# Output projection of an encoder block: seven half-size products in place of eight

## What is computed

```
y_ml = mlstm_group(q, k, v, o, ig, fg)            # [256, 1024]
y_ssm = mamba2_group(z, xbc, dt)                  # [256, 1024], normalised in 4 groups
mix = concat([y_ml, y_ssm], -1) @ w_out           # [256, 2048] @ [2048, 1024]
h = layer_norm(ALPHA * x + mix, ln1_g, ln1_b)
out = layer_norm(ALPHA * h + moe(h), ln2_g, ln2_b)
```

## Time and profile before

| | us |
|---|---|
| median of 3 runs | 746.25 (745.76 to 746.35) |
| profiled execution, span from its first to its last instruction | 744.0 |
| runs' median less that span (what lies around it) | 2.25 |
| TensorE busy | 713.8 (96%) |
| VectorE / ScalarE / GpSimd busy | 260.9 / 165.0 / 48.0 |
| data moved | 251.01 MB, 337 GB/s over the span |

### The profile page before, as it was taken

The page is one execution under the profiler, slowest core; times in us unless marked ns, Lnnn a source line. Parts: engine busy times, 40 slices in busy tenths (PEclk is TensorE's granted clock), DMA queues, the critical chain, the costliest instruction groups (busy, mean ns, idle before and its releaser), DMA issues.

```text
span 744.0 us, 11161 instructions
## 1 busy us (share of the span) xinstructions
PE 713.8 (96%) x4514; PEld 416.7 (56%) x4518; DVE 260.9 (35%) x639; ACT 165.0 (22%) x345; POOL 48.0 (6%) x65
## 2 busy tenths in 40 slices
PE   7999999999999999999999999999998999999993
PEld 6888888888864455445444435444443445444441
DVE  3401599657757085222112211022211122112225
ACT  1010423407940043111111111111111121111111
POOL 0120020320320020100000000000000000000000
PEclk9999999999999999999999999999999999999997
DMA  8964544544398548999999999999999999999993
GB/s 335 406 209 142 177 164 169 179 161 165 119 385 364 226 173 344 357 370 425 424 420 430 424 430 432 427 428 422 432 427 427 425 426 423 425 424 424 418 404 134
DMA packets 30946, 251.01 MB, mean 337 GB/s; under 512 B 4000, under 2 KB 4800, under 8 KB 10032
## 3 DMA queue, kind: packets, MB, share of 16 engines
q1 hardware_dynamic: 27792, 240.78, 79.4%
q0 software_dynamic: 2448, 8.48, 3.2%
q10 hardware_dynamic: 656, 1.05, 0.4%
HBM read 249.31 MB, written 1.11 MB: 337 GB/s over the span
## 4 chain that ended last, share of the span: by engine, by line
PE 72%; DMA 10%; DVE 9%; SPq 6%; issue 1%; ACT 1%; DVEq 0%
PE bank L1212 20%; PE bank L820 16%; DMA arena<-in_we_dram 10%; PE bank L1280 8%; PE bank L963 7%; PE bank L1131 7%; DVE arena L1603 5%; PE bank L1149 4%; SPq L627 3%; PE bank L934 1%; PE bank L900 1%; SPq L636 1%; PE bank L1254 1%; PE bank L1289 1%; ACT bank L1368 1%
## 5 line engine op out<-in xcount | busy, mean ns | idle before, releaser
L1212 PE MATMUL bank<-arena 128*64 128x512 f32 (+2 forms) x1008 | 198.8, 601 | 5.4 <-DMA arena<-in_we_dram 5.4
L820 PE MATMUL bank<-arena 128*128 128x256 f32 x768 | 167.7, 379 | 0.0
L820 PEld LDWEIGHTS bank<-arena 128*128 128x128 f32 x768 | 145.6, 190 | 20.5 <-issue 0.4
L1212 PEld LDWEIGHTS bank<-arena 128*64 128x64 f32 (+2 forms) x1008 | 57.7, 127 | 96.6 <-issue 94.0
L1280 PE MATMUL bank<-arena 128*64 128x512 f32 (+2 forms) x512 | 91.7, 584 | 3.5 <-DMA arena<-in_we_dram 2.1
L1131 PEld LDWEIGHTS bank<-onehotb,h_part 128*128 128x128 bf16 x1200 | 67.2, 98 | 19.4 <-issue 19.4
L1131 PE MATMUL bank<-onehotb,h_part 128*128 128x128 bf16 x1200 | 71.3, 219 | 0.0
L1928 DVE TENSOR_TENSOR y_lo<-bank,y_hi 128x512 fp32r<-128x512 f32 (+1 forms) x51 | 34.7, 681 | 101.9 <-ACT y_hi L1513 75.5
L1905 DVE TENSOR_REDUCE arena<-bank 64x1 f32<-64x3 f32 (+1 forms) x64 | 10.1, 158 | 160.8 <-PE bank L1230 160.2
L1280 PEld LDWEIGHTS bank<-arena 128*64 128x64 f32 (+1 forms) x512 | 26.3, 124 | 54.0 <-issue 44.6
L963 PE MATMUL bank<-arena 128*128 128x512 f32 x128 | 55.3, 592 | 0.0
(11 more groups left out here) (276 smaller groups left out, 493.6 us busy)
## 6 DMA issues: line engine op xcount, KB each, us to landing
arena<-in_we_dram SPq DMA_DIRECT2D x82, 1024.0 KB, 19.6
arena<-in_we_dram SPq DMA_DIRECT2D x17, 3072.0 KB, 30.8
arena<-in_we_dram SPq DMA_DIRECT2D x22, 2048.0 KB, 31.4
arena<-in_wc_dram SPq DMA_DIRECT2D x15, 1024.0 KB, 11.2
arena<-in_wn_dram SPq DMA_DIRECT2D x8, 1024.0 KB, 4.7
arena<-in_wo_dram SPq DMA_DIRECT2D x8, 1024.0 KB, 4.8
apart<-in_we_dram SPq DMA_DIRECT2D x7, 1024.0 KB, 29.7
arena<-decay_rows POOLq DMA_DIRECT2D x5, 1024.0 KB, 7.1
```

What stands on the lines that cost most here:

```text
L820: mm = nc.tensor.matmul(bank[n % 2][:, j * S:(j + 1) * S], wk, xk, start=(k == 0), stop=(k == KD - 1))
L1212: mm = nc.tensor.matmul(bank[0][rows[q], :], hc[v][:, k, rows[q]], place[at_q[part][q]][:, c:c + 512], start=(k == 0), stop=(k == KD - 1))
```

## The change

Each unit is read as a 2 x 2 block product: tokens' blocks A11, A12 (row block 0 and 1 of token block 0), A21, A22 (token block 1), and weight blocks B11, B12, B21, B22 (row block by column half). Seven products, each summed over the units in a bank of its own, take the place of the eight, in Winograd's form of Strassen's scheme: 1 = A11 B11, 2 = A12 B21, 3 = S4 B22, 4 = A22 T4, 5 = S1 T1, 6 = S2 T2, 7 = S3 T3.

GpSimd forms T1 to T4 (`weight_sums`): for units 0 and 1 between decay families 3 and 4, for 2 and 3 after families 3 and 4, for 4 to 7 behind the iota, each when unit m - 4 has been used. VectorE forms S1 to S4 (`token_sums`) for the mLSTM units before the variances and for the Mamba units before `layer_norm`, where the results are put together from the banks. TensorE's order: products 1 and 2 of units 0 to 3, the first sum of squares, the other five products unit by unit with the second sum of squares behind unit 0, then for units 4 to 7 product by product in the order 1, 2, 6, 5, 3, 7, 4.

The sums lie in places 20, 21, 8 and 15, so that those aren't loaded ahead of the projection's end; units 4 to 7 are loaded when product 3 is done.

```diff
+PROD = {1: bank[0], 2: bank[1], 3: bank[2], 4: bank[3], 5: bank[6], 6: bank[4], 7: bank[7]}
+ML_U = OUNITS // 2
+SUM_PLACES = (20, 21, 8, 15)
+sums_at = [place[i] for i in SUM_PLACES]
+DONE = {p: ML_U + 1 + i for i, p in enumerate((1, 2, 6, 5, 3, 7, 4))}
+def b_parts(m):
+    w, t = unit[m], sums_at[m % ML_U]
+    return ([w[:, i * 512:(i + 1) * 512] for i in range(4)], [w[:, 512:1024]] + [t[:, i * 512:(i + 1) * 512]
+                                                                               for i in range(3)])
+def a_sum(m, i):
+    return sums_at[m % ML_U][:, 1536 + (i - 1) * P:1536 + i * P]
+def a_part(m, block, t):
+    y = yT if m < ML_U else xbc
+    return y[:, 2 * m + block, t * P:(t + 1) * P]
...
     assert [home(STATIC_AT[c // 6], None, c % 6 // 2, c % 2) for c in range(PLACES)] == list(range(PLACES))
-    for c in range(20, PLACES):
-        load_first(c)
-    sp.wait_ge(decay_exp, 4 * NB)
-    load_first(8)
     sp.wait_ge(ssm_ready, 3)
     load_first(14)
     sp.wait_ge(ssm_ready, 4)
     load_first(13)
-    sp.wait_ge(decay_exp, FAMS * NB)
-    load_first(15)
     sp.wait_ge(y_ready, 1)
     load_first(16)
     load_first(19)
-    for u in range(4):
+    for u in range(ML_U):
         sp.wait_ge(mix_used, u + 1)
         load_first(u)
     load_first(12)
     sp.wait_ge(y_ssm, G)
     load_first(17)
-    sp.wait_ge(mix_used, 5)
-    load_first(4)
-    sp.wait_ge(mix_used, OUNITS)
-    for u in range(5, RING_U):
+    sp.wait_ge(mix_used, DONE[3])
+    for u in range(ML_U, OUNITS):
         load_first(u)
+    sp.wait_ge(mix_used, DONE[4])
+    for c in sorted(SUM_PLACES):
+        load_first(c)
     sp.wait_ge(h_ready, 2 * T)
     load_first(10)
     sp.wait_ge(logit_ready, T)
...
-    for fam in range(3, FAMS):
-        pool.wait_ge(decay_exp, (fam - 1) * NB)
-        decay_rows(fam)
+    pool_chain = [0]
+    def pool_link(ins):
+        ins.then_inc(s_pool, 1)
+        pool_chain[0] += 1
+        pool.wait_ge(s_pool, pool_chain[0])
+    def weight_sums(m):
+        u = CUNITS + RUNITS + m
+        pool.wait_ge(unit_full[u % RING_U], 16 * (u // RING_U + 1))
+        (b11, b12, b21, b22), (t1, t2, t3, t4) = b_parts(m)
+        pool_link(nc.gpsimd.tensor_tensor(t3, b22, b12, ALU.subtract))
+        pool_link(nc.gpsimd.tensor_tensor(t1, b12, b11, ALU.subtract))
+        pool_link(nc.gpsimd.tensor_tensor(t2, b22, t1, ALU.subtract))
+        nc.gpsimd.tensor_tensor(t4, t2, b21, ALU.subtract).then_inc(b_sums, 1)
+    pool.wait_ge(decay_exp, 2 * NB)
+    decay_rows(3)
+    weight_sums(0)
+    weight_sums(1)
+    pool.wait_ge(decay_exp, 3 * NB)
+    decay_rows(4)
     pool.wait_ge(rows_masked, 4 * FAMS)
     nc.gpsimd.tensor_scalar(nidentb, identb[:], -1.0, None, ALU.mult).then_inc(consts_ready, 1)
+    pool.wait_ge(decay_exp, 4 * NB)
+    weight_sums(2)
+    pool.wait_ge(decay_exp, FAMS * NB)
+    weight_sums(3)
     pool.wait_ge(ssm_ready, G)
     pool.dma_start(at(O_XPAD, 2 * D), a["ln"][:, 0:2 * D].to_broadcast([P, 2 * D])).then_inc(s_late, 16)
     for g in range(G):
...
+        weight_sums(m)
     halves = [slice(0, 512), slice(512, D)]
...
     for half in range(2):
         c = halves[half]
         pool.wait_ge(h_part1, 1 + half)
...
-    def project(k, t, halves=(0, 1)):
...
-    for m in range(4):
+    def squares(m):
+        if m == 0:
+            pe.wait_ge(consts_ready, 1)
+            pe.wait_ge(misc_evac, M_SQ)
+        else:
+            pe.wait_ge(misc_evac, M_SQ + 1)
+        pe.wait_ge(sq_sum, 2 * m + 2)
+        for i in range(2):
+            mm = nc.tensor.matmul(bank[5][:, i * S:(i + 1) * S], ones, zT[:, 4 * m + 2 * i, :],
+                                  start=True, stop=True)
+        mm.then_inc(misc_ready, 1)
+    def product(p, m):
+        (b11, _, b21, b22), (t1, t2, t3, t4) = b_parts(m)
+        by = {1: b11, 2: b21, 3: b22, 4: t4, 5: t1, 6: t2, 7: t3}[p]
+        y = {1: a_part(m, 0, 0), 2: a_part(m, 1, 0), 3: a_sum(m, 4), 4: a_part(m, 1, 1), 5: a_sum(m, 1),
+             6: a_sum(m, 2), 7: a_sum(m, 3)}[p]
+        return nc.tensor.matmul(PROD[p][:, :], y, by, start=(m == 0), stop=(m == OUNITS - 1))
+    for m in range(ML_U):
         y_transpose(m)
     pe.wait_ge(proj_evac, ZSTEP + 3)
+    for m in range(ML_U):
+        u = CUNITS + RUNITS + m
+        pe.wait_ge(unit_full[u % RING_U], 16 * (u // RING_U + 1))
+        pe.wait_ge(misc_evac, M_Y + m + 1)
+        for p in (1, 2):
+            product(p, m)
+    squares(0)
     pe.wait_ge(weight_ready, 5 * NB)
-    for k in range(SPLIT_K):
-        for t in range(T):
-            mm = project(k, t)
-        if k % 2 == 1:
-            mm.then_inc(mix_used, 1)
-        if k == SQUARES_AFTER:
-            pe.wait_ge(consts_ready, 1)
-            pe.wait_ge(sq_sum, G)
-            for m in range(2):
-                ps = misc(M_SQ + m)
-                for i in range(2):
-                    mm = nc.tensor.matmul(ps[:, i * S:(i + 1) * S], ones, zT[:, 4 * m + 2 * i, :],
-                                          start=True, stop=True)
-                mm.then_inc(misc_ready, 1)
-    for t, halves in ((0, (0, 1)), (1, (0,)), (1, (1,))):
-        for k in range(SPLIT_K, 2 * KD):
-            mm = project(k, t, halves)
+    pe.wait_ge(ssm_read, G)
+    for m in range(ML_U):
+        pe.wait_ge(b_sums, m + 1)
+        product(4, m)
+        if m == 0:
+            pe.wait_ge(y_ready, 2)
+        for p in (3, 5, 6):
+            product(p, m)
+        product(7, m).then_inc(mix_used, 1)
+        if m == 0:
+            squares(1)
+    for p in (1, 2, 6, 5, 3, 7, 4):
+        if p == 6:
+            pe.wait_ge(y_ready, 3)
+        for m in range(ML_U, OUNITS):
+            if p == 1:
+                u = CUNITS + RUNITS + m
+                pe.wait_ge(unit_full[u % RING_U], 16 * (u // RING_U + 1))
+                pe.wait_ge(y_ssm, m - ML_U + 1)
+            if p == 6:
+                pe.wait_ge(b_sums, m + 1)
+            mm = product(p, m)
         mm.then_inc(mix_used, 1)
     def transposes(t):
...
+    def token_sums(units):
+        for m in units:
+            ins = V.tensor_tensor(a_sum(m, 1), a_part(m, 0, 1), a_part(m, 1, 1), ALU.add)
+        link(ins)
+        for m in units:
+            V.tensor_tensor(a_sum(m, 3), a_part(m, 0, 0), a_part(m, 0, 1), ALU.subtract)
+        for m in units:
+            ins = V.tensor_tensor(a_sum(m, 2), a_sum(m, 1), a_part(m, 0, 0), ALU.subtract)
+        link(ins)
+        for m in units:
+            ins = V.tensor_tensor(a_sum(m, 4), a_part(m, 1, 0), a_sum(m, 2), ALU.subtract)
+        ins.then_inc(y_ready, 1)
+    dve.wait_ge(misc_evac, M_Y + 4)
+    token_sums(range(ML_U))
...
                         ).then_inc(misc_evac, 1)
     dve.wait_ge(misc_evac, M_SQ + 2)
     dve.wait_ge(y_gated, G)
...
+        h11, h12, h21, h22 = [h[:, t, n * 512:(n + 1) * 512] for t in range(T) for n in range(2)]
+        def from_x(to, t, n, by):
+            return V.scalar_tensor_tensor(out=to, in0=xin[:, t, n * 512:(n + 1) * 512], scalar=ALPHA, in1=by,
+                                          op0=ALU.mult, op1=ALU.add)
+        def plus(to, p, op=ALU.add):
+            return V.tensor_tensor(to, to, PROD[p][:, :], op)
+        dve.wait_ge(mix_used, DONE[1])
+        link(from_x(h11, 0, 0, PROD[1][:, :]))
+        dve.wait_ge(mix_used, DONE[2])
+        link(plus(h11, 2))
+        V.bn_stats(stat[:, 0, :], h11)
+        dve.wait_ge(mix_used, DONE[6])
+        link(V.tensor_copy(pair_sum, PROD[1][:, :]))
+        link(plus(pair_sum, 6))
+        from_x(h12, 0, 1, pair_sum)
+        from_x(h21, 1, 0, pair_sum)
+        link(from_x(h22, 1, 1, pair_sum))
+        dve.wait_ge(mix_used, DONE[5])
+        plus(h12, 5)
+        link(plus(h22, 5))
         for t in range(T):
-            for half in range(2):
-                dve.wait_ge(mix_used, MIXED[t][half])
-                c = slice(half * 512, (half + 1) * 512)
-                link(V.scalar_tensor_tensor(out=h[:, t, c], in0=xin[:, t, c], scalar=ALPHA,
-                                            in1=bank[2 * t + half][:, :], op0=ALU.mult, op1=ALU.add))
-                link(V.bn_stats(stat[:, 2 * t + half, :], h[:, t, c]))
+            if t == 0:
+                dve.wait_ge(mix_used, DONE[3])
+                link(plus(h12, 3))
+                link(V.bn_stats(stat[:, 1, :], h12))
+            else:
+                dve.wait_ge(mix_used, DONE[7])
+                plus(h21, 7)
+                link(plus(h22, 7))
+                V.bn_stats(stat[:, 3, :], h22)
+                dve.wait_ge(mix_used, DONE[4])
+                link(plus(h21, 4, ALU.subtract))
+                link(V.bn_stats(stat[:, 2, :], h21))
             link(V.bn_aggr(mv[:, t, :], stat[:, 2 * t:2 * t + 2, :].rearrange("p a b -> p (a b)")))
             V.tensor_scalar(vv[:, 0, t:t + 1], mv[:, t, 1:2], EPS, None, ALU.add).then_inc(var_ready, 1)
             dve.wait_ge(var_ready, 2 + t)
...
```

(19 more changed lines are left out.)

## The result

The changed kernel takes 752.81 us (752.42 to 753.64, 4 runs) against 746.0 for the kernel before (744.27 to 746.35, 4 runs): 0.91% more by the medians, the ratio of the runs 1.0102 with an interval of 1.0086 to 1.0119. Slower, as forecast, but by 6.8 us where the forecast had 3.8, and 0.3 us above the upper end of its own range. The profiled execution's span is 751.2, against 744.0.

What follows compares the result with a forecast made beforehand. Expert-weight transfers were taken to pace the kernel, their start hanging on the projection. Work +3.2 and transfers +4.8 gave +3.8 on the 744.0 span: 747.8, plus 2.25 for timed runs: 750.0 us, range 748.0 to 752.5, chance 0.6.

Steps and rivals of the forecast that it cites:

- What bounds the kernel, and the sign: Expert weights pace the kernel from about 330 us; the end follows their stream's start and remaining bytes; slower, chance 0.69.
- The mechanism: GpSimd's last sixteen sums and VectorE's chain take turns; y_ssm complete at 250.5, TensorE idle about 8 us before unit 6.
- wait of 1 to 2 us before product 6: Sign expected in TensorE's timeline: an idle 1 to 2 us before product 6, which must wait for the token sums.
- the end of the projection: Output projection on TensorE: token sums done at 254.9, twenty products (17.3 us) remain, so it ends at 272.2, 2.8 later.
- the clock: TensorE's lower clock after its idle stretch adds 1.7 us to product 2, covered by the wait for token sums until 254.9.
- the turns: VectorE's eight operations alternate with GpSimd's from 226.5: holds of 3.1 and 7.2 us, ending 5.9 late at 240.1.
- my walk: Step-by-step count of VectorE and GpSimd alternating from 226.5, giving y_ssm at 250.5 and token sums at 254.9.
- Behind the projection: Result assembly and normalisation after the projection: 0.4 us charged, routing 3.2 us late, its loads issued at about 294.
- The transfers: Late loads: -4.1 + 12.3 - 3.4 = +4.8 us against +3.2 for the work; up to 1.6 given back; 3.8 taken.
- VectorE hardly held up: Rival, chance 0.2: projection ends at 263.5 to 268.8, kernel at 741.5 to 746.7 us, middle 743.5.
- The whole instruction is held: Rival, chance 0.1: engines alternate for full instructions; y_ssm at 254.1, projection's end at 276.4, kernel 754.2 us.
- It comes out even: Rival, chance 0.1: four of VectorE's 8.7 us lost are saved, projection ends near 268.5, kernel about 746.5 us.

Runs made afterwards that it cites:

- e3: Kernel before the change, with the loads of places 8, 15, 20, 21 and unit 4 issued behind the projection; 749.88 us, ratio 1.0058.
- e1: Changed kernel without GpSimd's weight sums of units 4 to 7 (one 8-column operation per unit instead; doesn't compute the layer); 739.73 us, ratio 0.9918.
- e4: Changed kernel with ten idle products in TensorE's wait ahead of unit 6's product 1; 750.68 us, ratio 1.0066.
- v2: All 56 products, both sums of squares first, VectorE's chain with one PSUM operand, order 1, 2, 4, 6, 5, 3, 7; 745.68 us, ratio 1.0011.
- e7: Changed kernel with the 16 late GpSimd subtractions replaced by memsets (doesn't compute the layer); 741.02 us, a single execution.
- e2: Kernel before the change, with 16 linked GpSimd subtractions of 128x512 added behind the iota, result unread; 745.06 us, ratio 0.999.
- e6: Changed kernel with inverse roots in PSUM bank 5, so no VectorE Newton-step operation has both operands in SBUF; 746.63 us, ratio 1.0016.

## Why the prediction was right or wrong

**What bounds the kernel, and the sign.** Right. Against the profile before, the span moved with the first routed load in every run but e3, to within 1.7 us (e1: loads 4.6 us earlier, span 5.6 shorter; e4: 6.5 later, 4.8 longer; v2: 1.4 and 1.4). In e3 the loads were 0.6 late and the span 4.6 longer: there the bytes set it, the other half of what the prediction says. e1 and e7 show the time without the collision, in kernels that leave the late sums out.

**The mechanism.** Right, place and kind: VectorE's products waited a turn each, y_ssm was complete at 252.1 (forecast 250.5), TensorE stood 8.8 us (forecast about 8). e1 takes it away, e2 makes it in the old kernel, e6 leaves GpSimd's sums in place and takes it from the chain alone. One sign failed: there was no wait of 1 to 2 us before product 6.

**The step that failed** is the end of the projection: 272.2 forecast, 275.7 measured. 3.5 us of the 6.3 by which the projection is late were missing, and two terms make them up.

*First, the clock, 1.7 us.* I had found its price in the earlier trace rows and then set it at nothing, "covered" by the token sums' end at 254.9. That cover wasn't in my own numbers. Between unit 6's start at 249.6 and product 6 stand six products (product 1 of units 6 and 7, product 2 of four units), 5.2 us: product 6 would have come up at 254.8, and with the 1.7 at 256.5, 1.6 us behind the sums. The measured order is the same: the token sums took 3.6 us, not 4.4, and ended at 255.8; TensorE, at 1.2 GHz, came to product 6 at 258.4, and even at the upper level would have come at 256.7. So the 1.7 counted in full; e4 gives 1.8 of the projection's end back. (1.7 and 1.9 less the 0.1 by which 254.8 lies ahead of 254.9 are the 3.5.)

*Second, the turns, 1.9 us.* Unit 6 began at 251.5 in place of 249.6. GpSimd's subtraction of two float32 operands takes 1.26 to 1.28 alone (e6), not the 1.15 that I took from the earlier trace rows, where the second operand is a bfloat16 mask. One turn took 1.67 for a 512-wide operation and 1.40 for a 256-wide one (four scalings in 5.58); my walk had 1.57 and 1.31 (1.02 for GpSimd with 0.55 or 0.29). The walk also starts VectorE's first product at 229.8, though by its own count GpSimd's third operation runs to 230.1.

**Behind the projection** 0.4 was forecast and 0.9 measured (routing is 7.2 late, the projection 6.3): GpSimd's remainders of block 0, now late, meet block 1's normalisation, whose 1024-wide product takes 1.96 in place of 1.28. The same collision once more, in e1 and e7 too (1.97), which I had not looked for there.

```profile
277.94 1.96 DVE L1881 SCALAR_TENSOR_TENSOR arena<-arena,mv 128x1024 f32<-128x1024 f32 x1
```

**The transfers.** The arithmetic comes near. From product 3's end at 268.9 it gives -0.5 + 12.3 - 3.4 = 8.4. The stretch 295 to 330 gave 2.5 back (393 GB/s against 363, of 423), and 330 to 400 cost 0.7 (419 against 423): 6.6, where the span is 7.2 longer. The work alone says 7.2, so this run can't tell which of the two set the end. I had charged 0.6 above the work; here nothing was above it. In e3, where the work is only 0.6 late, the same sum gives 0.6 + 12.3 - 3.4 - 4.8 = 4.7 for a span 4.6 longer.

**The rivals.** *VectorE hardly held up*: e1 has its time (739.7, I had written 741.5), but only because it leaves GpSimd's sums out; with them VectorE was held up in every product. *The whole instruction is held*: its 276.4 is nearer to the measured 275.7 than my 272.2, but by luck: it leaves the clock out as mine does, and a pair of operations took 1.67 (231.14 to 232.81), not 0.69 + 1.28 = 1.97, so the rule as written isn't what brought it there. The rule in the Trainium skill (SBUF — State Buffer, "Who interferes with whom") on which operations contend is borne out by e6 and e7: two SBUF inputs against a GpSimd operation that reads, and the fast mode against one that writes; its "whole instruction" is some 0.3 us too much for each pair. *It comes out even*: no, the projection ended at 275.7.

## What to carry to other kernels

Work moved to an idle engine is free only if its operations don't take turns with the engine on the critical chain, or if that chain has slack (e2): look at both timelines in the same microseconds, and price each VectorE operation that reads two blocks of SBUF at one GpSimd operation more, less some 0.3 us. One operand in PSUM took a chain out of the turns here. A wait of some microseconds on TensorE is to be charged with the clock behind it (1.7 us behind 8.8), unless the next wait, with every product in front of it counted, ends later by more than that. Where a scheme saves products in some stretches at no cost, use it there alone: half of it gained 0.56%, the whole nothing.

## What the runs showed of the hardware that I had not expected

- A GpSimd two-operand operation of 128 x 512 took 1.26 to 1.28 us with two float32 operands (e6) and 1.15 with a bfloat16 second one, not held up by VectorE.
- In turns, operations overlapped by about 0.3 us a pair: 1.67 for 0.69 and 1.28.
- A VectorE operation of 512 with an operand or its result in PSUM ran at 0.69 to 0.70 beside GpSimd's subtractions; e6 moved the chain so, with one operation less in each half, and took it from 25.8 us to 14.6 (226.5 to 241.1).
- Beside memsets only the TENSOR_SCALAR was held up (0.43 to 0.72 and 0.82; e7, one execution).
- 20 records of products that nobody reads held TensorE's granted clock at 1.00 through a wait of 8.8 us; without them it was 0.50 in 245 to 250 (e4 and the changed kernel).
